# Prompt attention items between the digits of a key search, and sample value steps spread over the rest

## What is computed

```python
def _sparse_attend(q, qi, wi, ki_all, q_pos, n_keep, gather_kv):
    s = relu(einsum('bthd,bsd->bths', qi, ki_all))
    score = einsum('bths,bth->bts', s, wi) * IDX_SCALE
    score = where(key_pos <= q_pos, score, -inf)
    _, idx = top_k(score, n_keep)                 # prompt: 128 of 512, sample: 256 of 2049
    k_sel, v_sel = gather_kv(idx)
    logits = einsum('bthgd,btnhd->bthgn', qg, k_sel) * HEAD_DIM ** -0.5
    prob = softmax(where(sel_ok, logits, -inf))
    return einsum('bthgn,btnhd->bthgd', prob, v_sel)
```

## Time and profile before

| | |
|---|---|
| runs | 3971.18 us median of 3 (3961.3 to 3973.85) |
| profiled execution | 3966.45 us, span 3964.6 us |
| TensorE busy | 3665.7 us, 92% |
| VectorE busy | 2480.9 us, 63% |
| ScalarE busy | 1357.1 us, 34% |
| GpSimd busy | 1845.5 us, 47% |

### The profile page before, as it was taken

How to read it: one execution, slowest core, us unless ns; L and a number is a source line. 1 busy time by engine, 2 the same in 40 slices (tenths; PEclk the granted TensorE clock), 3 DMA queues, 4 the chain that set the end, 5 groups by cost and what they waited for, 6 DMA issues and landing times.

```text
span 3964.6 us, 63279 instructions
## 1 busy us (share of the span) xinstructions
PE 3665.7 (92%) x21581; PEld 3445.3 (87%) x21581; DVE 2480.9 (63%) x5090; ACT 1357.1 (34%) x1905; POOL 1845.5 (47%) x1118
## 2 busy tenths in 40 slices
PE   7899989999999999998888598989999999999998
PEld 7898989999899999998853357989898989999998
DVE  2352177878785777774556532286878785777773
ACT  2222244444444333333221233243434344333332
POOL 3333365555555555553520001465555555555551
PEclk9999999999999999999998799999999999999999
DMA  3212257777778999982235131256776788999992
GB/s 124 70 64 74 85 166 228 249 245 250 260 270 277 314 306 322 323 278 93 70 118 165 48 96 53 80 155 215 237 257 237 255 268 284 299 315 318 316 321 91
DMA packets 380003, 812.48 MB, mean 205 GB/s; under 512 B 33544, under 2 KB 239304, under 8 KB 372552
## 3 DMA queue, kind: packets, MB, share of 16 engines
q1 hardware_dynamic: 167024, 464.17, 33.5%
q0 software_dynamic: 61072, 221.08, 17.7%
q10 hardware_dynamic: 151696, 124.51, 10.6%
HBM read 696.90 MB, written 112.74 MB: 204 GB/s over the span
## 4 chain that ended last, share of the span: by engine, by line
PE 76%; DVE 10%; DMA 4%; issue 4%; ACT 3%; POOL 3%; SPq 1%; ACTq 1%; DVEq 0%; POOLq 0%
PE acc L558 47%; PE acc L545 15%; PE misc L680 3%; DMA rows<-u_in,expertP 3%; POOL w_lo L2025 2%; PE misc L903 1%; DVE hot_gate L1646 1%; DVE rows L1608 1%; PE acc L917 1%; ACT w_hi L998 1%; PE misc L845 1%; PE misc L940 1%; PE misc L720 1%; PE misc L568 1%; PE acc L929 1%
## 5 line engine op out<-in xcount | busy, mean ns | idle before, releaser
L2025 POOL TENSOR_TENSOR w_lo<-raw,w_hi 128x1024 fp32r<-128x1024 f32 x366 | 903.3, 2469 | 1410.7 <-ACT w_hi L998 1409.8
L558 PE MATMUL acc<-h_hi,w_hi 128*128 128x416 f32 x3072 | 1105.1, 360 | 58.5 <-POOL w_lo L2025 48.0
L558 PE MATMUL acc<-h_lo,w_hi 128*128 128x416 f32 x3072 | 1089.0, 354 | 0.0
L558 PE MATMUL acc<-h_hi,w_lo 128*128 128x416 f32 x3072 | 1081.8, 352 | 0.0
L998 ACT ACTIVATE w_hi<-raw 128x1024 fp32r<-128x1024 f32 x620 | 656.5, 1059 | 1158.1 <-PE acc L558 695.2
L558 PEld LDWEIGHTS acc<-h_hi,w_hi 128*128 128x128 f32 x3072 | 582.7, 190 | 85.5 <-issue 42.1
L558 PEld LDWEIGHTS acc<-h_hi,w_lo 128*128 128x128 f32 x3072 | 583.8, 190 | 6.5
L558 PEld LDWEIGHTS acc<-h_lo,w_hi 128*128 128x128 f32 x3072 | 583.4, 190 | 3.3
L1608 DVE CUSTOM_DVE_ANT_0 rows<-acc,rows 128x1024 f32<-128x1024 f32 (+1 forms) x224 | 273.3, 1223 | 243.7 <-DMA rows<-u_in,expertP 179.4
L1107 ACT ACTIVATE gelu<-acc 128x416 f32<-128x416 f32 x256 | 132.5, 518 | 756.6 <-PE acc L558 629.3
L545 PE MATMUL acc<-h_hi,w_hi 128*128 128x260 f32 x1472 | 309.6, 292 | 77.9 <-DVE h_lo L1415 30.2
(11 more groups left out here) (319 smaller groups left out, 5393.6 us busy)
## 6 DMA issues: line engine op xcount, KB each, us to landing
raw<-slabs_in SPq DMA_DIRECT2D x620, 512.0 KB
act_d<-gelu SPq DMA_DIRECT2D x256, 208.0 KB
gate_d<-gout SPq DMA_DIRECT2D x52, 1024.0 KB
abuf<-act_d ACTq DMA_DIRECT2D x32, 1664.0 KB
gbuf<-gate_d ACTq DMA_DIRECT2D x30, 1664.0 KB
unit<-cv_in SPq DMA_DIRECT2D x128, 128.0 KB, 2.0
unit<-ck_in SPq DMA_DIRECT2D x64, 160.0 KB, 3.1
unit<-ck_in ACTq DMA_DIRECT2D x64, 160.0 KB, 3.1
```

What stands on the lines that cost most here:

```text
L558: last = pe.matmul(acc[:, 0, par, 0:ND], w[:, c, :], m(c), start=c == 0 and w is w_hi[r] and m is m_hi, stop=c == KC - 1 and w is w_lo[r])
L2025: pool.tensor_tensor(w_lo[r % 2][:], raw[r][:], w_hi[r % 2][:].bitcast(F32), ALU.subtract).then_inc(lo_done, 1)
```

## The change

- The order of blocks is turned: item `i` is now block `3 - i // 16`.
- Items 0 to 16 run within the search. `BESIDE` is `[[0, 1], [2], [3, 4], [5], ..., [15, 16]]`, one list for each of the 11 digits. TensorE does the items of `BESIDE[k]` behind digit `k`'s product; VectorE does those of `BESIDE[k - 1]` between its hit for digit `k` and its wait for that digit, and the last two between the logits' maximum and the wait for the exponential. ScalarE's loop takes in the exponential of the sample's logits ahead of item 15.
- The transposes of the sample's logits (`turn_logits`, 5 groups) run two groups ahead of each of the items 19, 20 and 21 (`TURN_AT` is 19).
- The value steps stand behind items `VALUES_AT`: 21, 22, 24, 25, 27, 29, 30, 32, 34, 35, 37, 38, 40, 42, 43, 45, then each of 48 to 63.
- The digit's product goes to `misc[:, 3, 0:1]`, since the items use banks 0 and 1.

```diff
+BESIDE = []
+for _k in range(DIGITS):
+    _n = BESIDE[-1][-1] + 1 if BESIDE else 0
+    BESIDE.append([_n] if _k % 2 else [_n, _n + 1])
+TURN_AT = BESIDE[-1][-1] + 3
+VALUES_AT = [TURN_AT + 2 + i * 26 // 16 for i in range(16)] + [48 + i for i in range(16)]
...
-                for i in range(ITEMS + 4):
+                def beside(i):
                     if i >= NHEAD + 3 and (i - 3) % NHEAD == 0:
                         block_output((i - 3) // NHEAD - 1)
...
-                    if i % 2 and i < ITEMS:
-                        s_values(i // 2)
+
+                pe.wait_ge(prep_taken, 2)
+                pe.wait_ge(s_score_taken, NU + 1)
+                for k in range(DIGITS):
+                    digit_of(k)
+                    for i in BESIDE[k]:
+                        beside(i)
+                for i in range(BESIDE[-1][-1] + 1, ITEMS + 4):
+                    if TURN_AT <= i < TURN_AT + 3:
+                        for k in range(2 * (i - TURN_AT), min(2 * (i - TURN_AT) + 2, NU + 1)):
+                            turn_logits(k)
+                    beside(i)
+                    for k in range(STEPS):
+                        if VALUES_AT[k] == i:
+                            s_values(k)
...
                 for i in range(ITEMS + 4):
+                    if i == BESIDE[-1][0]:
+                        exp_logits()
+                    if TURN_AT <= i < TURN_AT + 3:
+                        for k in range(2 * (i - TURN_AT), min(2 * (i - TURN_AT) + 2, NU + 1)):
+                            take_turned_logits(k)
...
                     dve.tensor_scalar(hit[:], count[:], wanted, None, ALU.is_ge).then_inc(hit_ready, 1)
+                    if k:
+                        for i in BESIDE[k - 1]:
+                            beside(i)
                     dve.wait_ge(digit_done, k + 1)
...
                 dve.tensor_scalar(smx[:, 1:2], smx[:, 0:1], -(HD ** -0.5), None, ALU.mult).then_inc(s_max_done, 1)
+                for i in BESIDE[-1]:
+                    beside(i)
                 dve.wait_ge(s_exp_done, 1)
```

More of the change, by code:

```diff
@@ L924, in turn @@
                         pe.wait_ge(pT_done, i - 1)
-                    if b and h in (1, 2):
-                        pe.wait_ge(oT_lo, 2 * b)
+                    if p and h in (1, 2):
+                        pe.wait_ge(oT_lo, 2 * p)
                     for k in range(b + 1):
@@ L1324, in attention, with exp_logits, take_turned_logits @@
                 act.activation(v_tok[0:TS, 4, :], acc[0:TS, 0, 0, 0:2 * P], ACT.Copy).then_inc(prep_taken, 1)
[L1327 to L1330, removed]
+                def exp_logits():
+                    act.wait_ge(s_max_done, 1)
+                    act.activation(logits[:], logits[:], ACT.Exp, bias=smx[:, 1:2], scale=HD ** -0.5,
+                                   accum_out=smx[:, 2:3]).then_inc(s_exp_done, 1)
+                def take_turned_logits(k):
                     act.wait_ge(s_ptr_done, k + 1)
@@ L1852, in attention, with biased, output, beside @@
                 dve.sem_inc(prep_taken, 1)
+                def biased(i):
+                    b = 3 - i // NHEAD
+                    n = (b + 1) * P
+                    dve.wait_ge(log_done, i + 1)
+                    if i >= 4:
+                        dve.wait_ge(ptr_done, i - 3)
+                    dve.tensor_tensor_reduce(out=prob[i % 4][:, 0:n], in0=acc[:, 0, i % 2, 0:n], in1=idxs[:, b, 0:n],
+                                             scale=1.0, scalar=LOW, op0=ALU.add, op1=ALU.max,
+                                             accum_out=mx[:, i:i + 1]).then_inc(log_taken, 1)
+                    dve.wait_ge(log_taken, i + 1)
+                    dve.tensor_scalar(nmx[:, i:i + 1], mx[:, i:i + 1], -(HD ** -0.5), None, ALU.mult).then_inc(
+                        nmx_done, 1)
+                def output(i):
+                    p, h = divmod(i, NHEAD)
+                    dve.wait_ge(exp_done, i + 1)
+                    if p and h == 0:
+                        dve.wait_ge(oT_done, 2 * p)
+                    dve.reciprocal(rinv[:, i:i + 1], psums[:, i:i + 1]).then_inc(dve_step, step.up())
+                    dve.wait_ge(dve_step, step.at)
+                    dve.wait_ge(pv_done, i + 1)
+                    dve.tensor_scalar(o_tok[:, h * HD:(h + 1) * HD], misc[:, i % 2, 0:HD],
+                                      rinv[:, i:i + 1], None, ALU.mult).then_inc(o_done, 1)
+                def beside(i):
+                    if i >= NHEAD + 3 and (i - 3) % NHEAD == 0:
+                        p = (i - 3) // NHEAD - 1
+                        b = 3 - p
+                        for k in range(2):
+                            dve.wait_ge(oT_hi, 2 * p + k + 1)
+                            part = h_hi[:, 4 * k:4 * k + 4, b * P:(b + 1) * P]
+                            dve.tensor_tensor(h_lo[:, 4 * k:4 * k + 4, b * P:(b + 1) * P],
+                                              acc[:, 1, k, :].rearrange("p (k t) -> p k t", t=P), part.bitcast(F32),
+                                              ALU.subtract).then_inc(oT_lo, 1)
+                    if i < ITEMS:
+                        biased(i)
+                    if 3 <= i < ITEMS + 3:
+                        output(i - 3)
                 def ordered(op):
```

43 lines of the change are left out of this document (23 added, 20 removed).

## The result

The changed kernel took 3980.27 us, the median of 20 runs (3966.03 to 3989.39); the kernel before, run beside it, 3967.23 (20 runs, 3961.3 to 3975.71). The ratio is 1.0029, 95% interval 1.002 to 1.0038: slower by 0.29%, 11.5 us by the ratio and 13.0 by the medians. 3984 was forecast, with +13.1 over the kernel before.

What follows compares the result with a forecast made beforehand. TensorE, busy 92% of the span, bounds the kernel, but VectorE its search. Search +24.3 us and the way from last digit to projection -11.2 make +13.1, so 3984 us; range 3960 to 3999.

Steps and rivals of the forecast that it cites:

- The bound and the net: Whole kernel: VectorE bounds the search, TensorE the items; the change nets +13.1 us, giving 3984.
- the chances: Whole kernel: slower 0.47, within 0.3% (11.9 us) 0.43, faster 0.10.
- Part 1, the search: First to last digit: 17 items moved in make TensorE the bound at 1.2 GHz; 70.8 us against 46.5, +24.3.
- The rival of the rising clock: Search: bursts of items bring 2.4 GHz, so +11.7 us there and about 3965 in all; chance 0.13.
- The rival in which half clock outlasts the search: Value steps: 1.2 GHz lasts into them; +10 to +25 us, up to +56 more; chance 0.13.
- Part 2: Last digit to first value step: 15.0 us before, 32.5 after; 34 at 1.2 GHz, 30 if transposes raise the clock.
- Part 3: First to last value step: SyncE's page loads, 1.24 us each, become the bound; 143 us against 170.6 before.
- Part 4: Last value step to output projection: 13.5 us against 14.6, with cheaper trailing items and +1 for a possible half clock.

Runs made afterwards that it cites:

- kernel 1: The changed kernel with the value steps' page loads shared between SyncE and GpSimd; 3957.91 us, ratio 0.9974 to the kernel before.
- kernel 5: The changed kernel with twenty extra unused TensorE products before and beside the digits, to raise the clock; 3999.96 us, ratio 1.008 to the kernel before.
- kernel 7: The changed kernel with one item a digit, value steps spread evenly, and page loads shared between SyncE and GpSimd; 3963.98 us, ratio 0.9977.
- kernel 2: The changed kernel with one item beside each digit (11 instead of 17) and value steps spread evenly; 3963.58 us, ratio 0.9992 to the kernel before.
- kernel 3: The changed kernel with the old block order (block 0 first) and value steps spread evenly; 3953.89 us, ratio 0.9965 to the kernel before.
- kernel 9: kernel 3 with the page loads also shared between SyncE and GpSimd; 3956.68 us, ratio 0.9974 to the kernel before.

## Why the prediction was right

**The bound and the net.** Right. Forecast +13.1; the stretch shows +9.7 and +12.6 in the two executions, the runs +11.5 by the ratio and +13.0 by the medians. That the result sits at the edge between "no change" and "slower" is what the chances said. Two things made the numbers look better than the working. The errors of the parts had opposite signs: against the first execution the search was put 1.6 too low, and what follows it 5.0 too high. And the 3.7 us between 3984 and 3980.27 are the starting point: the kernel before stood at 3971.18 by three runs and at 3967.23 by twenty.

**Part 1, the search: +24.3, measured +25.9.** The mechanism held: grant 0.50 throughout, TensorE the bound, VectorE waiting. The mis-sized term is the item at half clock, 4.3 for a measured 4.64. Its logits took 2.00, where four products of another kind had suggested 1.75; transposes 0.91 as read; values 1.73, at the top of the 1.3 to 1.7. Hence 9.61 for the two-item digit, not 9.05 (the digit's product took 0.46, as read). What hid part of it: I put 6.0, 4.5 and 9.85 for the first two intervals and the long one before the ties, and 5.59, 4.21 and 9.64 were measured. One detail was named wrongly: VectorE's waits are seen at the items' output (9.8 us in 11 waits for the values) and at their logits (6.6 in 4), and not at the digit's product (0.8 in one), since the output stands ahead of the digit in VectorE's order.

**The rival of the rising clock: refuted for this kernel.** By the page's rule of the Trainium skill ("TensorE: Matmul & The Clock Gate", Part 1) sustained matmul activity releases the throttle. The trace doesn't agree: 64.94 of 72.40 us busy, 43.40 of them without a gap, all at 0.50. The grant is the same in the second execution and in kernel 1's. Its price was right: in the one execution with the clock up (kernel 5, with its extra products), the search took 57.2 us for the 58.2 worked out. So the half clock costs about 15.1 us here (72.3 - 57.2), or more, since the extra products are in the 57.2. That the clock could be had in this kernel was not shown.

**The rival in which half clock outlasts the search: refuted.** The grant is 1.00 over the first 90.9 us of the value steps, and the first of them takes 1.91 us.

**Part 2: 32.5, measured 29.1 and 29.8.** The exponential ended 8.4 us after the last digit (8.5 forecast; it takes 2.0 us, by the earlier trace rows too, where I wrote 2.2):

```profile
2241.34 2.01 ACT L1348 ACTIVATE logits<-logits,smx 128x2049 f32<-128x2049 f32 x1 [6.70 <-DVE smx L2018]
```

Then the clock rose in the run of transposes, the case for which the working had 30. I had mixed it with 34 us at half clock, so the term is 2.7 to 3.4 too high. That the clock can also stay down all the way is seen in kernel 7, with another placing (33.1 where kernel 2 has 25.6).

**Part 3: 143, measured 142.4 in both executions, and 142.2 and 142.9 in kernel 5's.** SyncE's 1.24 us a load is the bound, the waits begin near the 22nd step (the 23rd), and sharing the loads gave 20.1 of the 23 us that the working put between SyncE's 143 and TensorE's 120. The waits for pages were 12.9 us in sum, not 23. Most of the difference went into longer steps, since the grant fell (0.87 in the second stretch): TensorE was busy 127.2 us (88.61 + 38.56) instead of 118.6. Another 2.3 are the waits for VectorE at the ends of blocks, which the working left out. That changed no end, because SyncE set it. With the loads shared TensorE was busy 120.01 us at full clock, and with the same 2.3 of waits that makes the stretch of 122.3.

**Part 4: 13.5, measured 12.5 and 14.7.** Right within its working: the last step took 1.91 us in the first execution and 3.40 in the second.

**What the change would need.** Its idea was sound, its two choices were not. Dear items beside the digits ran at half clock (kernel 3 with cheap ones: +3.5 for +25.9), and the value steps drawn together ran into SyncE's issue (kernel 1: -20.1). Either correction alone makes it faster than before, by 0.35% (kernel 3, which also spaces the value steps evenly) and 0.26%. Both together (kernel 9) gave 0.26%, no more than either: kernel 3 has taken away most of the wait that the sharing cures.

## What to carry to other kernels

When work is moved beside an engine that is the bound, price it at the clock that holds there, not at the one where it ran before: put the cheapest items in the half-clock stretch and the dear ones where the clock is full. When work is taken away from a stage, compute what the queues behind it need per step (here four loads of 1.24 us) and see whether they become the bound; a queue that is "just ahead" has hidden its price. And compare executions over the stretch that the change touches, since the rest of this kernel moved by more than the effect.

## What the runs showed of the hardware

- TensorE, 90% busy for 72 us with products of 64 rows by 512 columns, transposes and 64-column products, was never granted more than 1.2 GHz in three profiled executions; in one of them 43.4 us of it have no gap.
- With twenty extra products the same program was granted 2.4 GHz in most of the search in one execution (two-item digit 5.85 us) and 1.2 GHz in another (11.54 us); the six timed executions of it were 22 to 35 us above the first one. What decides it is open.
- A wait of 2 us for a page can be followed by a step at half clock (2.08, then 3.39 us for 1.91), or by one at full clock (2.13, then 1.91).
- A page load issued by GpSimd takes 0.54 us of the engine, against 0.34 for SyncE's own instruction. Yet the loads come about as far apart on either, 1.23 and 1.24 us, since each engine reads the page number and prepares registers in between (the reading itself is 0.27 us on SyncE).
